# Issuing the modulation rows of a transformer layer from ScalarE on a second hardware queue, with SyncE left with TensorE's weights

## The reference

```
mod = c_act @ w_ada[l] + b_ada[l]
sh1, sc1, g1, sh2, sc2, g2 = [m[:, None, :] for m in jnp.split(mod, 6, axis=-1)]
h = rmsnorm(x, norm1_g[l]) * (1 + sc1) + sh1
qkv = h @ w_qkv[l]
...
x = x + g1 * y
h = rmsnorm(x, norm2_g[l]) * (1 + sc2) + sh2
x = x + g2 * hier_moe(h, ...)
```

## Time and profile before

| what | value |
|---|---|
| median of 3 runs | 1583.15 us (1582.28 to 1590.99) |
| the profiled execution's own time | 1584.59 us, its span 1582.8 us |
| TensorE busy | 1361.7 us, 86% of the span |
| VectorE busy | 652.2 us, 41% |
| ScalarE busy | 138.7 us, 9% |
| SP's hardware queue q1 | 567.64 MB in 94256 packets, 87.8% of the 16 engines' time |

### The profile page before, as it was taken

How to read it: one execution, slowest core, us unless ns; L and a number is a source line. 1 busy time by engine, 2 the same in 40 slices (tenths; PEclk the granted TensorE clock), 3 DMA queues, 4 the chain that set the end, 5 groups by cost and what they waited for, 6 DMA issues and landing times.

```text
span 1582.8 us, 14568 instructions
## 1 busy us (share of the span) xinstructions
PE 1361.7 (86%) x5720; PEld 690.4 (44%) x5720; DVE 652.2 (41%) x984; ACT 138.7 (9%) x390; POOL 48.2 (3%) x60
## 2 busy tenths in 40 slices
PE   2799998898898468998988988988988988988985
PEld 2678777566687355332332322332332332332321
DVE  4557676556575632224224224223223223233234
ACT  2110000146200011000000000000000000000001
POOL 0000000000100000000000000000000000000000
PEclk9899999959999789999999999999999999999998
DMA  9999999814498860999999999999999999999992
GB/s 334 397 361 401 394 362 359 323 69 160 141 392 324 314 266 27 376 425 428 424 426 429 424 425 430 424 425 429 424 425 429 424 425 430 424 425 430 424 424 85
DMA packets 96295, 572.10 MB, mean 361 GB/s; under 512 B 6048, under 2 KB 28752, under 8 KB 54400
## 3 DMA queue, kind: packets, MB, share of 16 engines
q1 hardware_dynamic: 94256, 567.64, 87.8%
q0 software_dynamic: 2000, 3.95, 0.9%
HBM read 569.38 MB, written 2.18 MB: 361 GB/s over the span
## 4 chain that ended last, share of the span: by engine, by line
PE 65%; DMA 24%; DVE 6%; issue 3%; ACT 1%; SPq 1%; DVEq 0%; POOL 0%; POOLq 0%; ACTq 0%
PE PS L1298 20%; DMA ring<-in_w_up 18%; PE PS L1319 10%; PE PS L1144 9%; PE PS L1278 8%; PE PS L1223 5%; PE PS L1149 3%; DMA ring<-in_w_ada 3%; DMA ring<-in_w_o 2%; PE PS L1260 2%; DVE W L761 2%; DVE W L1029 1%; PE PS L1094 1%; PE PS L1174 1%; PE PS L1194 1%
## 5 line engine op out<-in xcount | busy, mean ns | idle before, releaser
L1298 PE MATMUL PS<-ring,W 128*64 128x512 f32 x1024 | 239.0, 624 | 38.3 <-DMA ring<-in_w_up 38.1
L1319 PE MATMUL PS<-ring,W 128*64 128x512 f32 x1024 | 233.6, 610 | 27.4 <-DVE W L1029 17.7
L1298 PE MATMUL PS<-ring,gysq 128*64 128x512 f32 x1024 | 229.4, 604 | 15.9 <-DMA ring<-in_w_up 12.4
L1144 PE MATMUL PS<-r,ring 128*128 128x256 f32 x768 | 171.2, 386 | 9.2 <-DVE r L771 7.5
L1007 DVE TENSOR_TENSOR r<-r,PS 128x512 f32<-128x512 f32 x128 | 88.0, 688 | 200.5 <-PE PS L1278 200.5
L1298 PEld LDWEIGHTS PS<-ring,W 128*64 128x64 f32 x1024 | 81.2, 144 | 190.4 <-issue 190.4
L1144 PEld LDWEIGHTS PS<-r,ring 128*128 128x128 f32 x768 | 148.5, 194 | 32.6 <-DVE r L771 8.3
L761 DVE SCALAR_TENSOR_TENSOR W<-ring,sm,W 128x2048 f32<-128x2048 f32 x60 | 140.8, 2347 | 40.4 <-DMA ring<-in_w_ada 37.2
L1012 DVE TENSOR_SCALAR W<-W 128x256 f32<-128x256 f32 x32 | 22.0, 689 | 311.5 <-ACT W L660 311.5
L1298 PEld LDWEIGHTS PS<-ring,gysq 128*64 128x64 f32 x1024 | 78.6, 139 | 164.6 <-issue 164.6
L1319 PEld LDWEIGHTS PS<-ring,W 128*64 128x64 f32 x1024 | 76.2, 140 | 163.6 <-issue 144.0
(11 more groups left out here) (207 smaller groups left out, 737.3 us busy)
## 6 DMA issues: line engine op xcount, KB each, us to landing
ring<-in_w_gate SPq DMA_DIRECT2D x64, 2048.0 KB, 25.2
ring<-in_w_up SPq DMA_DIRECT2D x64, 2048.0 KB, 27.0
ring<-in_w_down SPq DMA_DIRECT2D x64, 2048.0 KB, 26.2
ring<-in_w_ada SPq DMA_DIRECT2D x32, 2048.0 KB, 15.4
ring<-in_w_qkv SPq DMA_DIRECT2D x17, 2048.0 KB, 16.7
ring<-in_w_ada SPq DMA_DIRECT2D x32, 1024.0 KB, 14.3
ring<-in_w_o SPq DMA_DIRECT2D x8, 2048.0 KB, 14.7
ring<-u_scr SPq DMA_DIRECT2D x2, 2048.0 KB, 19.8
```

Source lines behind the costliest of these rows:

```text
L1144: last = mm(ps[:, sub * T:(sub + 1) * T], w[:, t, (2 * b + sub) * P:(2 * b + sub + 1) * P], hT[:, QT * q + t, :], start=(t == 0), stop=(t ...
L1298: last = mm(PS[64 * j:64 * j + 64, i % 2, :].rearrange("p (m n) -> p m n", m=2), hE[i % 2][:, k], w[:, :, t, 256 * j:256 * j + 256], start ...
L1319: last = mm(PS[64 * q:64 * q + 64, 4 + i2, :], hidT[:, b, 64 * j:64 * j + 64], w[:, b, 512 * ch:512 * ch + 512], start=(j + b == 0), stop= ...
```

## The change

ScalarE issues 28 of the chunks of `w_ada` itself: `ada(1,..)`, `ada(2,..)`, `ada(3,..)`, and the 16 chunks `adv(2,..)` and `adv(3,..)` (parts G1 and SH2). They are the plan's entries, in its order, with the same slots and the same waits; only the issuing engine and so the queue differ. `ada(0,..)` and the last 16 `adv` chunks stay on SP. The transfers are placed among ScalarE's work: four chunks ahead of `affine(0)`, six among the copies of pass 0, six behind them, then `affine(2)`, seven, `affine(3)`, and the last five.

```diff
+        rows_in = [n for n, item in enumerate(order) if item[2] in ("ada", "adv")]
+        BY_ACT = rows_in[4:QT * 4 + 2 * ADA_CHUNKS]
...
-            for kind, i, _, s in order:
+            for n, item in enumerate(order):
+                kind, i, _, s = item
+                if n in BY_ACT:
+                    continue
...
-                if kind == "ada":
-                    q, k = i
-                    rows4 = here.rearrange("p (t a n) -> p t a n", t=4, a=2)
-                    for a in (SH1, SC1):
-                        n0 = a * D + q * QC
-                        load(s, turn if a == SH1 else 1, rows4[:, :, a], ada_v[:, 4 * k:4 * k + 4, n0:n0 + QC])
-                elif kind == "adv":
-                    src = ada_v[:, 2 * i[1]:2 * i[1] + 2, i[0] * D:(i[0] + 1) * D]
-                    load(s, turn, here.rearrange("p (t n) -> p t n", t=2), src)
+                if kind in ("ada", "adv"):
+                    modulation(sp, item)
...
+            queue = iter(BY_ACT)
+
+            def fetch(count):
+
+                for _ in range(count):
+                    modulation(act, order[next(queue)])
+
+            fetch(4)
             affine(0)
             for k in range(4):
                 if k == 3:
...
                     else:
                         A.activation(value(b), ps, ACT.Copy).then_inc(qkv_ok, 1)
+                    if n in (3, 5, 8, 10, 12, 14):
+                        fetch(1)
+            fetch(6)
             affine(2)
+            fetch(7)
             affine(3)
+            for n in queue:
+                modulation(act, order[n])
             act.wait_ge(qb_ps, QT * QB + 1)
```

More of the change, by code:

```diff
@@ L364, in value, with read_by, load @@
             return v_sb[:, b // 2, P + b % 2 * 512:P + b % 2 * 512 + 512]
+        def read_by(eng, who, count):
+            s, each = {"pe": (pe_chunk, WO_STEP), "qkv": (qb_ps, 4), "ada": (first_ok, 4), "adv": (accd, 2),
+                       "bias": (lg_ok, NH // 2), "x": (xr_ok, 1)}[who]
+            eng.wait_ge(s, QT * QB + 1 if who == "qkv" and count == QKV_CHUNKS else each * count)
+        def load(eng, s, turn, dst, src):
+            if turn > 1:
+                read_by(eng, *held[s][turn - 2])
+            eng.dma_start(dst, src).then_inc(landed[s], 16)
+        def modulation(eng, item):
+            kind, i, _, s = item
+            here, turn = slot(s), number[kind, i][1]
+            if kind == "ada":
+                q, k = i
+                rows4 = here.rearrange("p (t a n) -> p t a n", t=4, a=2)
+                for a in (SH1, SC1):
+                    n0 = a * D + q * QC
+                    load(eng, s, turn if a == SH1 else 1, rows4[:, :, a], ada_v[:, 4 * k:4 * k + 4, n0:n0 + QC])
+            else:
+                src = ada_v[:, 2 * i[1]:2 * i[1] + 2, i[0] * D:(i[0] + 1) * D]
+                load(eng, s, turn, here.rearrange("p (t n) -> p t n", t=2), src)
+        rows_in = [n for n, item in enumerate(order) if item[2] in ("ada", "adv")]
+        BY_ACT = rows_in[4:QT * 4 + 2 * ADA_CHUNKS]
         @block.sync
@@ L409, in _ @@
                     if q == QT:
-                        load(s, turn, here.rearrange("p (t n) -> p t n", t=KT), qkv_v[:, :, NHA * HD:NHA * HD + CW])
+                        load(sp, s, turn, here.rearrange("p (t n) -> p t n", t=KT), qkv_v[:, :, NHA * HD:NHA * HD + CW])
                     else:
-                        load(s, turn, here.rearrange("p (t n) -> p t n", t=QT),
+                        load(sp, s, turn, here.rearrange("p (t n) -> p t n", t=QT),
                              qkv_v[:, QT * q:QT * q + QT, COLS[k]:COLS[k] + 1024])
@@ L418, in _ @@
                     src = bass.AP(u_scr.tensor, u_scr.offset + i * 16 * UL, [[1, P], [UL, 16], [1, T]])
-                    load(s, turn, here.rearrange("p (h k) -> p h k", h=16), src)
+                    load(sp, s, turn, here.rearrange("p (h k) -> p h k", h=16), src)
                 elif kind == "x":
-                    load(s, turn, here.rearrange("p (h n) -> p h n", h=H), x_v)
+                    load(sp, s, turn, here.rearrange("p (h n) -> p h n", h=H), x_v)
                 else:
-                    load(s, turn, here.rearrange("p (t n) -> p t n", t=KT), wo_v[:, :, i * CW:(i + 1) * CW])
+                    load(sp, s, turn, here.rearrange("p (t n) -> p t n", t=KT), wo_v[:, :, i * CW:(i + 1) * CW])
             def expert_chunk(e, k, s):
```

## The result

The changed kernel took 1592.32 us (median of 10 runs, 1588.41 to 1596.48) beside 1583.68 us for the kernel before in the same sessions (10 runs). The ratio is 1.0054, 95% interval 1.0034 to 1.0075: slower by 8.6 us, a small loss, but with an interval that does not reach 1. 1591.0 had been forecast. The profiled execution took 1590.01 us, with a span of 1588.3.

A forecast was written before the change was run, and what follows sets the result against it. TensorE was taken to bound the four passes, whose end moves the kernel's end. 17.1 (start) + 1.3 (clock) - 10.6 (idle times) = +7.8 us, so 1591.0 us, chance 0.40; its own range 1587 to 1595, overall 1572 to 1599.

The forecast's parts named there:

- The start of pass 0: Ahead of `affine(0)`: eight issues hold ScalarE in a full queue, so pass 0 starts at 69.2 instead of 52.1 us.
- The turn itself: Both hardware queues ahead of pass 0: engines take a packet of each in turn, giving the 17.1 us later start.
- Equal bytes: Rival, chance 0.22: queues get equal bytes ahead of pass 0, which starts 11.0 us later; +1.7, 1584.9 us.
- ScalarE isn't held: Rival, chance 0.17: the second queue takes all eight issues ahead of `affine(0)`; only the gain stays, -10.6, 1572.5 us.
- two terms of the sum: Ahead of `affine(0)`: SP's 1600 packets left to move, and 2048 of ScalarE's moved when the eighth issue ends.
- The clock: Start of pass 0: TensorE idles longer, up to five us at half speed instead of two; +1.3 us, bounds 0 and 2.5.
- The idle times: TensorE's waits in passes 2 and 3 (1.44 and 6.08 us) and the slow stretch go; 10.6 us gained.
- The rival by which they stay: Rival, chance 0.16: transfers, not their order, set the passes' pace, so idle times stay; up to +18.4, 1601.6 us.
- its milder form: The same rival with pass 3's idle time gone: +9.6, 1592.8 us.
- a shift of the passes' end moves the end of the kernel by as much: Stages behind the passes hang on their end; passes were to end about 8 us later than 291.5.
- All stages behind of the same length: Sign of being right: every stage behind the passes keeps its length.
- The waits inside pass 0: ScalarE's issues among pass 0's copies are hidden, their waits met; if one isn't, PSUM banks cover 10 us.

The follow-up runs named there:

- the three versions above: Changed kernel with all four chunks behind `affine(0)`, 1575.62 us; `ada(1,..)` on SP and ScalarE's first three chunks later, 1576.84; kernel before, SP's list reordered, 1578.41.
- the second profile of the kernel before: The kernel before, unchanged, profiled once more: one run of 1585.09 us, passes' end at 289.85.
- the eight transfers alone: Against the changed kernel, ScalarE issues only the four chunks ahead of `affine(0)`, the other 24 are back in SP's list: 1601.63 us, ratio 1.0113.
- the run on one queue: The kernel before with two pairs of chunks moved ahead of `qkv` chunks in SP's one list: 1578.41 us, ratio 0.9976.

## Why the prediction was right

- **The start of pass 0.** Forecast 17.1 us later, by a queue that holds four such transfers and engines that take the queues' packets in turn: the eighth issue was to end at 68.0 and ended at 68.28; pass 0 started at 69.55 for 69.2. The turn itself, chosen without a row, is shown: 330 packets each. Equal bytes was the rival that this refutes, and "ScalarE isn't held" falls with the issue of 7.55 us. That the end came out within 0.3 us is partly luck, since two terms of the sum were off and cancelled. SP's queue still had some 1430 packets to move from 41.7 us on, and not 1600; and about 2470 of ScalarE's packets had been moved when the eighth issue ended, and not 2048 (in bytes of both queues 10.6 MB, for 10.7 forecast). The seventh and eighth issue lasted 2.48 and 2.58 us, where 5 to 8 was forecast: SP's queue was nearly empty by then. "Holds four such transfers" is thus a rough figure: when the fourth, fifth, sixth and eighth issue ended, 1540 to 1720 of the packets issued were still to be moved.
- **The clock.** 1.3 us were set down, 0.85 measured as pass 0's extra length, inside the bounds of 0 and 2.5. The prediction has the clock low until 54 us in the kernel before; its own row, 0.52 from 54 to 55, says until 55. And the reason given, that TensorE idles for longer, is not shown: pass 0 took 59.69, 59.90 and 59.98 us in the three versions above that start it at 52.1 to 52.4 with its 192 matmuls in one row of over 44 us, and there TensorE had idled no longer than before.
- **The idle times.** Forecast to go, worth 10.6 us: 1.70 + 8.99 = 10.69. The rival by which they stay is refuted by TensorE's rows, not by the time: its milder form, with only pass 3's gap gone, gave 1592.8, which is nearer to the measured 1592.32 than the forecast. But pass 2 took 57.06 us, all of it busy. Of its 1.70 us, though, some may be chance: the gap was 0.48 in the second profile of the kernel before, and with the eight transfers alone, in the old order, pass 2 took 57.46 us. The engines ran at 404 and 409 GB/s in passes 1 and 2, about the 405 that a pass of 56.96 us needs, so they were near their limit and kept up. The rule of the Trainium skill (DMA: Bandwidth & Descriptors, "Issuing engines are not separate DMA queues"), that issuing on several engines saves only the sequencer's time to issue, agrees with the run on one queue: nothing was gained by the second queue as such.
- **The stages behind.** The step "a shift of the passes' end moves the end of the kernel by as much" holds in the medians (+8.6 for +7.6), not within one profile: the profiled span grew by 5.5 only, chiefly since the attention took 97.30 us for 100.59 at a granted clock of 0.84 for 0.79 (the projection and the routing behind it took 1.4 us more). "All stages behind of the same length" was thus wrong for a single profile. The scatter of that stage was not foreseen.
- **The waits inside pass 0.** None held ScalarE, as forecast; no copy of pass 0 came late. What the forecast left out is that these issues compete with SP's rows by packet. In the changed kernel all the `ada(1,..)` transfers were on ScalarE's own queue ahead of them, so it didn't show; with them on SP it cost 4.0 us.

## What to carry to other kernels

An issuing instruction is not free when its queue is full: it holds its engine until there is room (7.0, 7.6 and 6.9 us here), so a prefetch that may find the queue full belongs behind the last instruction that something else waits for, not ahead of it, even by one line. When transfers wait in one list for different readers, look first whether the slow reader's wait stands ahead of the fast one's; reordering the list may do what a second queue does. And where two queues ran together, the one with larger packets got more of the bytes (two thirds with packets of twice the size, four fifths with four times), so don't start its transfers before they are needed.

## What the runs showed of the hardware that was not expected

Queues take turns by packets and not by bytes, whichever has the larger ones: 330 to 330 packets for 1.34 to 0.68 MB, and 176 to 177 packets for 0.34 to 1.33 MB.

The limit of a queue goes by packets, not by transfers or bytes. Of transfers of 512 packets the fourth was held, though they were of 1 MB each. In the kernel before, `qkv(4,0)`, one transfer of 2048 packets of 1 KB, went into an empty queue in 0.37 us, and the very next one, `adv(3,1)`, was held for 2.26 us. On the other side, the kernel before issues six transfers of the experts' weights in a row, 2 MB each, and the last of them

```profile
554.35 0.60 SPq L440 DMA_DIRECT2D ring<-in_w_up  x1
```

is not held, though the five ahead of it, 10 MB, had been issued in the 6.7 us before, in which the engines moved 2.26 MB. Their packets are of 16 KB, 128 to a transfer, as the 1.2 us behind 552.6 show:

```profile
DMA packets 32, 0.52 MB, mean 437 GB/s; under 512 B 0, under 2 KB 0, under 8 KB 0
```

The attention's length followed the granted clock from 0.71 to 0.89 in kernels with the same instructions there, by up to 15.6 us.
